# One expert weight pair loaded before the attention, and a projection moved from expert passes 1 to 8 to passes 22 to 29

## The reference

```
u    = rmsnorm(h);  proj = u @ w_in
kc, vc = compress(k), compress(v)      # gelu(blocks @ w_cmp1) @ w_cmp2
h    = h + concat(norm(nsa_attention), norm(fox_attention)) @ w_out
x    = rmsnorm(h)
       # 32 experts, 4 for each token, by a router
h    = h + sum over the token's experts of weight * (swiglu(x @ w_up + b_up) @ w_down + b_down)
h    = h + (p @ w_ple) * sigmoid(rmsnorm(h) @ w_ple_gate)
out  = rmsnorm(h)
```

## Time and profile before

| | |
|---|---|
| median of 3 runs | 1893.15 us |
| the profiled execution | 1892.56 us |
| its span | 1890.4 us |
| PE busy | 1810.5 us (96%) |
| PE weight loads | 1230.1 us (65%) |
| DVE, ACT, POOL busy | 748.5, 613.6, 85.7 us |
| mean granted TensorE clock | 0.99 |
| DMA | 580.33 MB, mean 307 GB/s |
| expert pairs | 192 of 2 MiB, 17.2 us from issue to landing (median) |

### The profile page before, as it was taken

One profiled execution on the slowest core, in us unless ns is written; L12 is line 12 of the kernel. 1 busy time (PEld: TensorE's weight loads), 2 busy tenths in 40 slices (PEclk: granted clock), 3 DMA queues, 4 the chain that ended last, 5 costly groups with the idle time before them and its releaser, 6 DMA issues.

```text
span 1890.4 us, 29803 instructions
## 1 busy us (share of the span) xinstructions
PE 1810.5 (96%) x12122; PEld 1230.1 (65%) x12122; DVE 748.5 (40%) x1566; ACT 613.6 (32%) x1096; POOL 85.7 (5%) x104
## 2 busy tenths in 40 slices
PE   6999999999999999999999999999999999999997
PEld 4855899999989999968544444444444444444446
DVE  2575577656577745375321111211211121121117
ACT  3456455444455536365211111111111111111115
POOL 0010111000111100100000000000000000000002
PEclk8999999999999999979999999999999999999999
DMA  9638645555455554403999999999999999999992
GB/s 394 256 151 344 249 170 185 181 199 216 165 223 181 179 203 145 158 1 108 422 427 425 426 425 424 427 425 427 425 416 395 424 428 425 427 426 425 428 423 98
DMA packets 63828, 580.33 MB, mean 307 GB/s; under 512 B 5904, under 2 KB 9232, under 8 KB 10352
## 3 DMA queue, kind: packets, MB, share of 16 engines
q1 hardware_dynamic: 63296, 577.17, 75.2%
q10 hardware_dynamic: 432, 1.71, 0.3%
HBM read 577.81 MB, written 1.05 MB: 306 GB/s over the span
## 4 chain that ended last, share of the span: by engine, by line
PE 59%; DMA 19%; DVE 12%; ACT 7%; issue 2%; SPq 0%; ACTq 0%; POOL 0%; DVEq 0%
PE ps L2541 18%; DMA ring<-in_experts 17%; PE ps L2552 6%; DVE wd_lo L1235 6%; ACT wd_hi L731 5%; PE ps L2464 3%; PE ps L1960 3%; PE ps L1956 3%; PE ps L1957 3%; PE ps L2241 2%; PE ps L2236 2%; PE ps L2237 2%; DMA ring<-in_weights 2%; PE ps L2564 2%; PE ps L2015 1%
## 5 line engine op out<-in xcount | busy, mean ns | idle before, releaser
L2541 PE MATMUL ps<-ring,A 128*64 128x512 f32 x2048 | 453.2, 595 | 22.4 <-DMA ring<-in_experts 21.7
L2541 PEld LDWEIGHTS ps<-ring,A 128*64 128x64 f32 x2048 | 154.5, 137 | 292.8 <-issue 291.9
L1808 DVE TENSOR_TENSOR A<-ps,W 128x512 f32<-128x512 f32 x64 | 44.3, 692 | 743.0 <-PE ps L2531 743.0
L1235 DVE TENSOR_TENSOR wd_lo<-ring,wd_hi 128x2048 fp32r<-128x2048 f32 x107 | 245.1, 2294 | 183.1 <-ACT wd_hi L731 183.1
L1956 PE MATMUL ps<-aL_hi,wd_hi 128*128 128x256 f32 x1040 | 256.7, 284 | 3.7 <-ACT wd_hi L731 2.0
L1957 PE MATMUL ps<-aL_lo,wd_hi 128*128 128x256 f32 x1040 | 254.9, 283 | 0.0
L731 ACT ACTIVATE wd_hi<-ring 128x2048 fp32r<-128x2048 f32 x107 | 203.9, 1906 | 119.2 <-PE ps L2241 69.8
L2552 PE MATMUL ps<-ring,A 128*64 128x512 f32 x1024 | 227.0, 595 | 0.0
L1956 PEld LDWEIGHTS ps<-aL_hi,wd_hi 128*128 128x128 f32 x1040 | 199.4, 192 | 6.7 <-issue 5.5
L1957 PEld LDWEIGHTS ps<-aL_lo,wd_hi 128*128 128x128 f32 x1040 | 199.5, 192 | 0.1
L1062 ACT ACTIVATE A<-ps 128x512 f32<-128x512 f32 x64 | 38.2, 597 | 407.7 <-PE ps L2541 388.1
(11 more groups left out here) (395 smaller groups left out, 2219.2 us busy)
## 6 DMA issues: line engine op xcount, KB each, us to landing
ring<-in_experts SPq DMA_DIRECT2D x192, 2048.0 KB, 17.2
ring<-in_weights SPq DMA_DIRECT2D x161, 1024.0 KB, 5.1
hT<-in_x SPq DMA_DIRECT2D x1, 1024.0 KB, 7.6
hT<-in_ctx SPq DMA_DIRECT2D x1, 1024.0 KB, 17.0
hT<-in_weights SPq DMA_DIRECT2D x1, 1024.0 KB, 5.9
tab<-in_tables ACTq DMA_DIRECT2D x1, 768.0 KB, 9.2
out<-aT SPq DMA_DIRECT2D x2, 384.0 KB, 2.5
A<-in_tables SPq DMA_DIRECT2D x1, 548.0 KB, 5.8
```

Of the source, the lines that this page charges most:

```text
L1235: dve.tensor_tensor(wd_lo[:, b], cell(PLAN[name]["first"][k]["cell"]), wd_hi[:, b].bitcast(F32), ALU.subtract).then_inc(split_lo, 1)
L1808: dve.tensor_tensor(m_gl[:, j].rearrange("p c h n -> p (c h) n"), ps[:, TURN_BANKS[j], :].rearrange("p (c n) -> p c n", c=8), b_up[:, 8 * ...
L2541: mm = pe.matmul(ps[h * CAP:(h + 1) * CAP, 4 + j, :], xg[:, c, :], w[:, c, h], start=(c == 0), stop=(c == KC - 1))
```

## The change

SP loads pair 1 of the first expert behind the four `w_out` loads, once the compression has read cells 2 and 3, ahead of the wait for the attention's end; `expert_weights` leaves it out for that expert. The definitions of the rows and of `load_pair` move up with it. p's projection goes from passes 1 to 8 to passes 22 to 29. The start flag of the first combine, which hung on tile 0, becomes an argument of its own, `opens`. On PE, pass 1 is written out, 2 to 14 and 18 to 21 are loops, 22 to 29 and 30 are written out; on ACT, 1 to 14 and 17 to 21 are loops.

```diff
-        TURNED = 9
+        P_PASSES = range(22, 30)
...
+            EARLY = 1
+
+            def early_pair():
+                sp.wait_ge(cmp_proj, 2)
+                load_pair(EARLY, 0)
...
             stream("cmp")
             stream("w_out")
+            early_pair()
 
             sp.wait_ge(b_o, 12)
             sp.wait_ge(b_out, 8)
...
             def expert_weights():
                 for m in range(MPAIRS):
+                    if m == EARLY:
+                        continue
...
 (ACT)
                     one(0, 0, True)
-                    for p in range(1, TURNED):
-                        one(p, p, tile=p - 1)
-                    with act.Fori(TURNED, CROWDED - 1) as p:
+                    with act.Fori(1, CROWDED - 1) as p:
                         one(p, p)
...
-                    with act.Fori(CROWDED + 1, PASSES - 1) as p:
+                    with act.Fori(CROWDED + 1, P_PASSES[0]) as p:
                         one(p, p)
+                    for tile, p in enumerate(P_PASSES):
+                        one(p, p, tile=tile)
+                    one(PASSES - 2, PASSES - 2)
                     one(PASSES - 1, PASSES - 1, last=True)
...
 (PE)
-                        combine(p, tile == 0)
+                        combine(p, opens)
...
                     one(0, 0, True)
-                    for p in range(1, TURNED):
-                        one(p, p, tile=p - 1)
-                    with pe.Fori(TURNED, CROWDED - 1) as p:
+                    one(1, 1, opens=True)
+                    with pe.Fori(2, CROWDED - 1) as p:
                         one(p, p)
...
-                    with pe.Fori(CROWDED + 2, PASSES - 1) as p:
+                    with pe.Fori(CROWDED + 2, P_PASSES[0]) as p:
                         one(p, p)
+                    for tile, p in enumerate(P_PASSES):
+                        one(p, p, tile=tile)
+                    one(PASSES - 2, PASSES - 2)
                     one(PASSES - 1, PASSES - 1, last=True)
```

More of the change, by code:

```diff
@@ L564, in stream, with load_pair @@
                 run(name, 0, PLAN[name]["items"])
+            up_rows = wmoe.rearrange("(g b) (i r) n -> g (b i) (r n)", b=2, r=2)
+            down_rows = wmoe.rearrange("(g b) p n -> g p b n", b=2)
+            def load_pair(m, e):
+                into = ring[:, 2 * m * CELL:2 * (m + 1) * CELL]
+                if m < UP_PAIRS:
+                    sp.dma_start(into, up_rows[m + e * MPAIRS]).then_inc(pair_landed[m], 16)
+                else:
+                    sp.dma_start(into.rearrange("p (b n) -> p b n", b=2), down_rows[m + e * MPAIRS]).then_inc(pair_landed[m], 16)
+            EARLY = 1
+            def early_pair():
+                sp.wait_ge(cmp_proj, 2)
+                load_pair(EARLY, 0)
             sp.dma_start(hT[:, :, 0:T], x_d).then_inc(h_in, 16)
@@ L586, in _ @@
             sp.dma_start(hT[:, :, T:TT], wdense[PLAN["w_ple"]["source"]].rearrange("p (k n) -> p k n", k=KC)).then_inc(p_in, 16)
[L588 to L596, removed]
             def pair_fed(m):
@@ L2568, in combine, with one @@
                     mm.then_inc(moe["comb"], 1)
-                def one(p, e, first=False, tile=None, last=False, crowded=False, wide_next=False, behind=False):
+                def one(p, e, first=False, opens=False, tile=None, last=False, crowded=False, wide_next=False, behind=False):
                     pe.wait_ge(moe["xg"], since(M, "xg") + p + 1)
```

## The result

The changed kernel takes 1897.61 us (median of 9 runs, 1896.1 to 1900.57) against 1893.15 of the kernel before, run beside it. The ratio is 1.0018, with a 95% interval of 1.0009 to 1.0026. The prediction was 1892.1 us, with a range that ended at 1895.0.

What follows compares the result with a forecast made beforehand. The expert stage, half the time, was taken as bound by one DMA stream of weight pairs. The restart gave -1.1 us, all other terms 0 (fetches -1.6 + 1.6), so 1893.15 became 1892.1 us, range 1889.5 to 1895.0.

Steps and rivals of the forecast that it cites:

- The tail: Behind pass 31: last combine and tail start when their data is there, as before; cost 0, upper bound 0.5 us.
- The restart of the stream: Pass 1's first pair meets an empty DMA queue and lands 7.7 us after issue; -1.1 us, bounds 0 and 1.7.
- The attention: The early pair's transfer beside the attention, where DMA idles, delays nothing; 0, bounds 0 and 4.9 us.
- Passes 1 to 8: Without the projection TensorE gains 1.83 us a pass, which becomes waiting for data from pass 4 or 5; worth 0.
- The fetches: Instruction fetches leave passes 1 to 8 (-1.6 us) and return in 22 to 29 (+1.6); net 0, bounds -1.6 and +1.1.
- The crowded pass: Pass 16: TensorE comes waiting for data in both kernels, the stream stops for the same 4.4 us; no change.
- Passes 22 to 29: With the projection, each takes TensorE 1.83 us more where it idles 1.53; cost 0, upper bound 0.5 us.
- TensorE's lag: Passes 22 to 29: TensorE falls up to 0.4 us behind the data, 0.1 more over 8 passes; pass 30 wins 1.82.
- A: Start of pass 1: the stream never stops, so the whole pair is saved, 4.92 us, giving 1888.2 us; chance 0.10.
- C: Passes 22 to 29: fetches cost less there than in early passes; 1.1 + 1.6 us saved, 1890.5 us; chance 0.16.
- B: Written-out passes 22 to 29: each instruction fetch stalls TensorE; +6.8 us, giving 1900.0 us; chance 0.05.

Runs made afterwards that it cites:

- The half alone: The kernel before with only the early load of the first expert's pair, p's projection left in passes 1 to 8: 1893.93 us, ratio 1.0000.

## Why the prediction was wrong, step by step

- **The tail**: "Pass 31, the last combine and the tail then start when their data is there, as before. Cost 0; upper bound 0.5." This step failed, and with it the sign. The data is there (DVE at 1854.81 to 1855.29), but TensorE doesn't go on: 2.6 us of idle time and a clock at 0.50 behind it, 3.15 us in all. Taking the branch away gives back 2.6 of them by the traces and 3.1 by the medians; moving the code by 30, 40 or 64 instructions brings the gap to the kernel before. I had counted the instructions that the change adds as DMA packets only, and not asked what lies behind them. That the jump's target had still to be fetched is my reading of the gap; no trace shows which blocks had been fetched. It is the written-out passes that moved the branch into the gap.
- **The restart of the stream**: forecast -1.1 us from a landing of 7.7; the landing took 9.1, so the pair landed at 927.7 where, shifted by the 0.47, the kernel before has 927.4: **+0.3**. The mechanism held (918.57 as bound by up(0), the queue at a share of 0.00 ahead of it, some 4 us of the saved transfer turned into idle time); the size was that of one landing. Other kernels with the early pair had 7.7 (two), 8.3, 8.5 and 9.0 (two). The half alone measures 1.0000. By the trace the 4.92 us saved are all gone.
- **The attention**: forecast 0. The end of the attention came 0.47 us later in this execution. Executions of kernels without padding differ by up to 2.5 us at the experts' first issue (888.27 to 890.78), so this says nothing.
- **Passes 1 to 8**: right. TensorE waits for data from pass 4 (the first wait at 1021.49), and 223.20 of 231.24 us are busy. The fetches gone from here were to bring 1.6; from 888 to pass 12 it won 0.98, with the restart's 0.3 against it 1.3.
- **The crowded pass**: right (0.92 again).
- **Passes 22 to 29**: the forecast had 1.6 us for the fetches and up to 0.5 for TensorE's lag, repaid in pass 30. Measured 1.9 up to pass 30 (238.10 for 236.17), 1.7 up to pass 31: some 1.5 of written-out code, some 0.4 of projection, 0.24 repaid.
- **Rivals**: A (4.9 us saved) and C (fetches cheaper late) didn't happen. B had what I take for the cause, the supply of instructions, at the wrong place and with the wrong size (+6.8): it looked for stalls in each written-out pass, where there are none, and not at the one jump forward. It had 0.05.

The medians differ by 4.5 us, the spans by 4.0. Of these, 3.15 are the gap, and the rest, 0.85, is within what single executions differ by.

## What to carry to other kernels

Code that is written out or rolled up moves everything behind it: look for the next jump over unused code, and put independent work ahead of it (2.8 us came back here). Moving a transfer of 4.92 us ahead won nothing here, since the transfer behind it hung on a product that hung on the router (918.57 for 918.13): ask whether that one can start earlier as well. And padding to move code must stand where it costs nothing, or only its trace can be read.

## What the runs showed of the hardware

- At the branch over the code for further passes TensorE stood idle for 2.64 us in the changed kernel, 2.50 with the projection alone and 2.44 in the changed kernel with 128 more instructions; in the kernel before for 2.62, 3.01 and 2.53 us with 64, 40 and 30 more. Without the projection it was 0.65 us, and nothing in the kernel before, with the early pair alone and in the changed kernel with 144 more. In the kernel before a packet of the instruction queue starts there as well (1852.23), and TensorE's dummies run from 1852.00 to 1854.43 without a pause.
- Behind the 2.64 us without a matmul the granted clock was 0.50 from 1856 to 1859 in the changed kernel, where it had been 1.00; from 1860 on it was at 1.00 again. In the five other kernels with 2.44 to 3.01 us it fell to 0.50 as well; in the one with 0.65 us it stayed at 1.00.
- Looped passes fetched nothing: the kernel before has no packet of the instruction queue from 1200 to 1360 and from 1550 to 1830. Its trace has 2568 records of TensorE in the eight passes from 1565.63 to 1801.80, 321 a pass, more than the 253 of a packet.
- Eight passes with 10 fetches of 16 KB beside a full queue took 237.66 us, 1.5 more than eight without (236.17), and more than the fetches' share of 0.3% of 238 us (0.7 us).
- Pairs of 2 MiB issued into an idle queue landed after 7.6 to 9.1 us.
- With 288 waits already met, 144 instructions in the trace, TensorE's first matmul starts at 16.81 us; in the changed kernel it does at 9.12 and in the kernel before at 8.97.
